# Window-cache copies as 64 quarter parts issued from ScalarE's program, row reads left to GpSimd's queue

## The chip, the cores and the metric

One core of a Trainium2 chip runs the whole kernel. The metric is the device time in microseconds. The kernel has no second core to wait for, so what is read below is one core's engines and its 16 DMA engines.

## What is computed

The reference is one inference step of a decoder layer on 256 prompt tokens and 8 sample tokens (D = 2048), all in float32:

```
q, k, v, u = RMSNorm(x) @ w_in                    # 12 heads x 64, and 1280 pooled channels
attn = merge over 3 dilated windows; for the samples the keys and values are
       rows of cache_win_k / cache_win_v (8 x 2048 x 768 floats each)
x += [attn | pooled u @ pool_w] @ w_out
x += cross-attention(4 heads x 128) over 256 memory tokens (w_ck, w_cv, w_cq, w_co)
x += MoE: top 1 of 4 groups, top 2 of 8 experts, 32 experts with 3 weights of 4 MB each
outputs: y, the new rows, and win_k_sample / win_v_sample =
         the two caches shifted by one row, the new row behind them
```

What matters here is the last line. Rows 1 to 2047 of each sample's cache are copied to rows 0 to 2046 of the output, from device memory to device memory: 2 x 8 copies of 6.29 MB, 100.6 MB in all. No computation reads these outputs, apart from the new last row, which the sample's score reads back.

## The kernel before

It is written by hand, one program per engine, with semaphores. SyncE (SP) issues all the weights into a ring of two 4 MB slots and a third slot: `big(i)` (L403 to L418) waits until piece i-2 has been used by TensorE (`piece_used`) and then loads piece i. The pieces are w_ck, w_cv, seven of w_in, pool_w, four of w_out, w_cq and w_co. A piece of w_in is loaded as rows of 2,048 bytes, w_co and w_e_down as rows of 8,192 bytes, w_e_gate and w_e_up as rows of 16,384 bytes.

The stages of TensorE's program, in order: transposes of the memory tokens and of x; the projection onto w_ck and w_cv (`project`, L668, sample rows L674); five pieces of w_in with `project`; then `channels(j)` (L742) for ten groups of channels, between which the prompt's attention runs pair by pair (scores L771, `turn_probs` L780, values L789); the samples' values (L873) and the pooling map (L863); sixteen output tiles against w_out (L895), each with a transpose of a sample's memory keys (L902); cross-attention (L914 to L980); the projection onto w_co (L1014) with the router; and then 32 experts (`expert(i)`, L1054 to L1138). The experts' weights are used once each. An expert's gate and up weights lie in the two ring slots, and those of the next expert can be loaded into a slot only when TensorE has used it.

GpSimd issues everything else that comes from the caches, in one queue in which transfers start in the order of issue. `window_rows` (L557 to L562) reads the 321 rows of one sample that attention needs, `key_rows(b)` (double buffered) and `value_rows(b)` (three buffers) call it, `memory_rows` (L578) reads 256 rows of a memory cache, and `cache_copy(i)` (L551 to L555) copies one sample's keys or values as 96 rows of 65,504 bytes:

```
src = a[("cache_win_k", "cache_win_v")[kv]][0, b, 1:WB].rearrange("s h e -> (s h e)")
pool.dma_start(dst.rearrange("(p f) -> p f", p=96), src.rearrange("(p f) -> p f", p=96)).then_inc(copied, 16)
```

The order in GpSimd's program is written out by hand: five copies, each when another weight piece has landed (`piece_landed`); then the key rows of samples 0 and 1; and from there on a copy after every second or third batch of rows, again behind a wait for a landed piece. So a batch of rows can stand in the queue behind a copy that was issued just before it. VectorE's `sample_scores(b)` (L1526 to L1530) waits for a batch of key rows; it stands between `enter(p)` and `normalise(p)`, for which TensorE's `turn_probs(p)` waits.

ScalarE issues no DMA. It evacuates banks, squares and takes exponentials; its order against TensorE is set by `A_ORDER`, VectorE's by `V_ORDER` (four banks each).

Of the kernel before, what the change touches and what calls it, by code (L numbers as in the profile page):

```python
# [11 lines left out]
ALU = mybir.AluOpType  # L12
# [120 lines left out]
V_ORDER = (["gains"] + ["mem"] * 8 + ["bias"] * 2 + ["scale"] + ["ck", "cv", "in", "in"] + ["flip"] * 6 + ["in"] * 3  # L133
           + ["score"] * 12 + ["sscore"] * 2 + ["state", "svals"] + ["out"] * KT + ["cq"] * 4 + ["xscore"] * 4
           + ["xsscore", "ssum", "logits", "pos"])
A_ORDER = (["x"] * 16 + ["ck", "cv"] + ["mk"] * 2 + ["in", "sin"] * 5
# [12 lines left out]
def hybrid_decoder_layer(nc, a):  # L149
    with ExitStack() as ctx:  # L150
# [168 lines left out]
        copied = sem("copied")  # L319
# [81 lines left out]
        def _(sp):  # L401
# [29 lines left out]
            for dst, src in ((rb[0:NBUCKET], a["rel_bias"]), (ohp[0:33], cc("ohp", 33)), (ohs[0:33], cc("ohs", 33)),  # L431
                             (tri[:], cc("tri")), (flip, cc("flip")), (moec[:], cc("moe")), (corr[:], cc("corr")),
                             (poolsc[:].rearrange("p g b -> p (g b)"), cc("pools")), (sel[:], cc("sel"))):
                sp.dma_start(dst, src).then_inc(const_landed, 16)  # L434
            sp.wait_ge(zeros_ready, 1)
            for i in range(4):
                sp.dma_start(rbs[0:NBUCKET, i, 0:H], a["rel_bias"]).then_inc(const_landed, 16)
            for i, g in enumerate(("q_norm_g", "k_norm_g")):
                sp.dma_start(gqk[:, i, :], a[g].to_broadcast([P, HD])).then_inc(const_landed, 16)
            sp.dma_start(gck[:, 0, :], a["ck_norm_g"].to_broadcast([P, XD])).then_inc(const_landed, 16)  # L440
            sp.dma_start(b36[:, 0:NG], a["b_rg"].to_broadcast([P, NG])).then_inc(const_landed, 16)
            sp.dma_start(gE[:], a["norm_ffn_g"][0].rearrange("(p k) -> p k", k=KT)).then_inc(const_landed, 16)
# [98 lines left out]
            sp.wait_ge(copied, (2 * NB + 1) * 16)  # L541
# [7 lines left out]
        def _(pool):  # L549

            def cache_copy(i):  # L551
                b, kv = i // 2, i % 2
                src = a[("cache_win_k", "cache_win_v")[kv]][0, b, 1:WB].rearrange("s h e -> (s h e)")
                dst = a[("win_k_sample", "win_v_sample")[kv]][0, b, 0:WB - 1].rearrange("s h e -> (s h e)")
                pool.dma_start(dst.rearrange("(p f) -> p f", p=96), src.rearrange("(p f) -> p f", p=96)).then_inc(copied, 16)  # L555
# [24 lines left out]
            for i in range(5):  # L580
                piece_landed(pool, CV + i)
                cache_copy(i)
# [13 lines left out]
            piece_landed(pool, IN0 + 6)  # L596
            cache_copy(7)
            key_rows(7)
# [6 lines left out]
            piece_landed(pool, POOLW)  # L605
            pool.wait_ge(state_landed, 16)
            cache_copy(8)
            for b in range(3, NB):
                value_rows(b)
            pool.dma_start(a["pool_sample"][0, :, 0:HIST - 1], a["state_pool"][0, :, 1:HIST]).then_inc(copied, 16)  # L610
# [24 lines left out]
            for i in range(14, 16):  # L635
                pool.wait_ge(gu_landed[0], 32)
                cache_copy(i)
# [1316 lines left out]
```

## Time and profile before

| | |
|---|---|
| time, median of 3 runs | 1636.61 us (1635.2 to 1639.62) |
| the profiled execution's own time | 1635.73 us |
| its span, first to last instruction | 1633.9 us |
| busy: TensorE, VectorE, ScalarE, GpSimd | 1262.8, 559.4, 190.1, 58.7 us |
| DMA: bytes, mean rate | 608.79 MB, 373 GB/s |

The span is that of one profiled execution, and the sum of the prediction is made against that execution's time. Busy times overlap each other. In the views below a DMA share is the mean busy share of the 16 DMA engines; it can come out a few per cent above 1, because records that start inside a stretch are counted whole and short ones overlap. The "chain" follows the work that ended last back through what released it, in order of time.

### The profile page before, as it was taken

The page shows a single profiled execution, that of the slowest core. Times are in us where ns is not written, and L with a number is a line of the kernel's source. Part 1 is how long each engine was busy: PE and PEld are TensorE (multiplying, and loading weights), DVE is VectorE, ACT ScalarE, POOL GpSimd, SP SyncE. Part 2 cuts the span into 40 slices and gives each one's busy share as a digit, 9 for nine tenths or more (in the row PEclk, how much of TensorE's full clock was granted, in tenths as well). Part 3 has the DMA queues.
Part 4 walks back from the last instruction along what each step waited for, and adds up shares of the span by engine and source line. Part 5 has one row for each costly group of instructions (what it writes and reads, how often), then busy time and mean ns, then how long its engine had stood idle before and what let it go on. Part 6 is the DMA issues. An engine that isn't in the chain of part 4 may idle for free.

```text
span 1633.9 us, 23554 instructions
## 1 busy us (share of the span) xinstructions
PE 1262.8 (77%) x10061; PEld 654.2 (40%) x10061; DVE 559.4 (34%) x1154; ACT 190.1 (12%) x463; POOL 58.7 (4%) x109
## 2 busy tenths in 40 slices
PE   5999997579998789777777767767767676777676
PEld 3444466465777676432222222222222222222222
DVE  2200153453000142444333433333334343343444
ACT  4000012221110122300000000000000000000000
POOL 0000021112110000000000000000000000000000
PEclk8999998788999899889898998998989899899898
DMA  8999899999889699989999999999999999999995
GB/s 317 308 338 309 309 330 354 313 289 293 286 313 331 228 349 379 356 334 405 428 426 425 428 427 425 426 426 427 428 424 427 426 427 427 424 428 427 425 427 238
DMA packets 85187, 608.79 MB, mean 373 GB/s; under 512 B 10914, under 2 KB 14523, under 8 KB 49529
## 3 DMA queue, kind: packets, MB, share of 16 engines
q1 hardware_dynamic: 76521, 479.68, 72.1%
q0 software_dynamic: 8624, 128.51, 23.4%
q8 instruction: 32, 0.52, 0.1%
q14 instruction: 10, 0.08, 0.0%
HBM read 603.15 MB, written 106.18 MB: 434 GB/s over the span
## 4 chain that ended last, share of the span: by engine, by line
DMA 55%; PE 36%; DVE 4%; SPq 2%; issue 1%; ACT 1%; POOL 0%; DVEq 0%; ACTq 0%
DMA ring<-in_w_e_up_dram 43%; PE pb L1113 11%; PE pb L668 10%; DMA Z<-sample_queries 3%; DMA qkm<-in_cache_mem_k_dram 3%; PE pb L895 3%; DMA ring<-in_w_in_dram 3%; DMA ring<-in_w_out_dram 3%; PE pb L914 2%; PE pb L1014 2%; SPq L434 1%; PE pb L863 1%; PE pb L742 1%; PE pb L674 1%; SPq L494 1%
## 5 line engine op out<-in xcount | busy, mean ns | idle before, releaser
L1113 PE MATMUL pb<-ring,xT 128*32 128x256 f32 x4096 | 312.0, 472 | 196.4 <-DMA ring<-in_w_e_up_dram 195.8
L1884 DVE TENSOR_TENSOR Z<-pb,Z 128x512 f32<-128x512 f32 (+1 forms) x384 | 237.6, 679 | 390.3 <-PE pb L1078 390.3
L1113 PEld LDWEIGHTS pb<-ring,xT 128*32 128x32 f32 x4096 | 154.3, 134 | 377.3 <-DMA ring<-in_w_e_up_dram 246.9
L668 PE MATMUL pb<-ring,hreg 128*128 128x512 f32 (+1 forms) x320 | 125.3, 551 | 0.0
L1138 PE MATMUL pb<-ring,xT 128*32 128x512 f32 x992 | 112.9, 595 | 0.0
L1078 PE MATMUL pb<-xT 32*128 32x512 f32 (+1 forms) x768 | 106.0, 622 | 3.6 <-issue 1.9
L1054 PE MATMUL pb<-Z,xT 128*32 128x512 f32 (+1 forms) x792 | 100.5, 622 | 3.0 <-DVE xT L1863 3.0
L742 PE MATMUL pb<-hreg,ring 128*128 128x264 f32 x320 | 77.2, 402 | 10.9 <-DMA ring<-in_w_in_dram 10.9
L668 PEld LDWEIGHTS pb<-ring,hreg 128*128 128x128 f32 x320 | 60.3, 190 | 61.9 <-issue 60.2
L895 PE MATMUL pb<-hreg,ring 128*128 128x264 f32 x320 | 78.1, 402 | 0.3 <-ACT Z L1307 0.3
L742 PEld LDWEIGHTS pb<-hreg,ring 128*128 128x128 f32 x320 | 62.7, 199 | 24.5 <-DMA ring<-in_w_in_dram 11.3
L1408 ACT ACTIVATE xT<-pb 128x128 f32<-128x128 f32 x32 | 8.9, 278 | 524.9 <-PE pb L1113 524.9
L895 PEld LDWEIGHTS pb<-hreg,ring 128*128 128x128 f32 x320 | 62.6, 200 | 11.1 <-issue 0.4
L1896 DVE TENSOR_SCALAR xT<-xT 128x128 f32<-128x128 f32 x32 | 7.3, 227 | 158.4 <-ACT xT L1408 158.4
L668 PE MATMUL pb<-ring 128*128 128x512 f32 x128 | 57.7, 614 | 0.0
L1657 DVE TENSOR_TENSOR xT<-pb,xT 128x264 f32<-128x264 f32 x16 | 6.9, 433 | 134.9 <-PE pb L895 134.9
L1138 PEld LDWEIGHTS pb<-ring,xT 128*32 128x32 f32 x992 | 29.1, 109 | 56.3 <-issue 55.6
L895 PE MATMUL pb<-Z,ring 128*128 128x264 f32 x192 | 45.3, 386 | 0.0
L1054 PEld LDWEIGHTS pb<-Z,xT 128*32 128x32 f32 (+1 forms) x792 | 19.3, 109 | 57.5 <-issue 53.6
L1119 PE MATMUL pb<-ident,xT 128*128 128x128 f32 x32 | 10.5, 328 | 40.9 <-DVE xT L1902 40.9
L1062 PE MATMUL pb<-ident,xT 128*128 128x128 f32 x132 | 21.2, 284 | 26.1 <-ACT xT L1404 26.1
L895 PEld LDWEIGHTS pb<-Z,ring 128*128 128x128 f32 x192 | 36.5, 190 | 6.2
(302 smaller groups left out, 1059.9 us busy)
## 6 DMA issues: line engine op xcount, KB each, us to landing
ring<-in_w_e_gate_dram SPq DMA_DIRECT2D x64, 2048.0 KB, 19.0
ring<-in_w_e_up_dram SPq DMA_DIRECT2D x64, 2048.0 KB, 23.5
ring<-in_w_e_down_dram SPq DMA_DIRECT2D x31, 4096.0 KB, 22.0
out_win_k_sample_dram<-in_cache_win_k_dram POOLq DMA_DIRECT2D x8, 6141.0 KB, 23.9
out_win_v_sample_dram<-in_cache_win_v_dram POOLq DMA_DIRECT2D x8, 6141.0 KB, 22.2
ring<-in_w_in_dram SPq DMA_DIRECT2D x7, 4096.0 KB, 22.3
ring<-in_w_out_dram SPq DMA_DIRECT2D x4, 4096.0 KB, 22.2
ring<-in_cache_win_k_dram POOLq DMA_DIRECT2D x16, 288.0 KB, 19.1
```

The source lines that it names most:

```text
L434: sp.dma_start(dst, src).then_inc(const_landed, 16)
L668: last = mm(bk[:, 0:n], xt[:, k, tile * P:tile * P + P], w[:, k, 0:n], start=(k == 0), stop=(k == KT - 1))
L742: last = mm(bk[:, 0:TOK], w[:, k, :], hT[:, k, :], start=(k == 0), stop=(k == KT - 1))
L895: last = mm(bk[:, 0:TOK], w[:, k, :], mix(k), start=(i == 0), stop=(i == KT - 1))
L914: last = mm(bk[:, 0:TOK], wk(CQ)[:, k, XD * h:XD * h + XD], hT[:, k, :], start=(k == 0), stop=(k == KT - 1))
L1014: last = mm(pb[o % 4][:, 0:TOK], wo[:, h, P * o:P * o + P], oT[:, h, :], start=(h == 0), stop=(h == XH - 1))
L1054: last = mm(pb[0][32 * c:32 * c + 32, :], pick[0:n, t, :], xn[0:n, t, 512 * c:512 * c + 512], start=(t == 0), stop=(t == 2))
L1062: last = nc.tensor.transpose(pb[0][:, P * j:P * j + P], xe[:, P * j:P * j + P], ident[:])
L1078: last = mm(banks[c][0:n, :], GT[r, P * t:P * t + n], yo[r, :], start=True, stop=True)
L1113: last = mm(pb[1][32 * c:32 * c + 32, 0:256], XT[:, k % 4, 32 * (k // 4):32 * (k // 4) + 32], w[:, :, k8, P * c:P * c + P], start=(k == 0) ...
L1138: last = mm(pb[3][32 * c:32 * c + 32, :], aT[:, 32 * f:32 * f + 32], w[f][:, 512 * c:512 * c + 512], start=(f == 0), stop=(f == 3))
L1884: last = V.tensor_tensor(d, banks[c][0:n, :], d, ALU.add)
```

## The change

All the cache copies leave GpSimd's program. They are cut in quarters: 64 parts, each 32 rows of 49,128 bytes (1.57 MB), contiguous in source and destination, and are issued from ScalarE's program, with no wait of their own, at points that are spread over everything before the experts:

```diff
+            def cache_part(n=1):
+                nonlocal parts
+                for _ in range(n):
+                    b, kv, q = parts // 8, parts // 4 % 2, parts % 4
+                    parts += 1
...
+                    r = slice((WB - 1) * AW // 4 * q, (WB - 1) * AW // 4 * (q + 1))
+                    act.dma_start(dst[r].rearrange("(p f) -> p f", p=32), src[r].rearrange("(p f) -> p f", p=32)).then_inc(copied, 16)
```

The places are: 1 part after the first w_ck tile is evacuated, 2 within the sixteen copies of x, 2 after w_cv's tile, 1 after the memory keys; 4 per w_in piece for n = 0 to 3 (two after `in`, two after `sin`) and 2 for n = 4; 6 in `channels` (j = 1, 2, 3, 5, 7, 9); 2 in the map loop; 13 in the output loop; 9 in cross-attention; 8 in the loop over w_co's tiles, and 2 behind the last `rows_back`.

GpSimd's program keeps its row reads in the same order and with the same waits as before, less the copies and the waits for pieces. At its start it gets the 18 small constant loads that were SyncE's:

```diff
             for t in range(2):
                 sp.dma_start(memr[:, t], a["mem_prompt"][0, P * t:P * t + P]).then_inc(mem_landed[t], 16)
+            big(CK)
             for t in range(2):
                 sp.dma_start(xraw[:, t], a["x_prompt"][0, P * t:P * t + P]).then_inc(x_landed[t], 16)
             sp.dma_start(xraw[0:NB, 2], a["x_sample"][:, 0]).then_inc(x_landed[2], 16)
-            big(CK)
-            for dst, src in ((rb[0:NBUCKET], a["rel_bias"]), (ohp[0:33], cc("ohp", 33)), (ohs[0:33], cc("ohs", 33)),
...
             big(CV)
```
```diff
-            for i in range(5):
-                piece_landed(pool, CV + i)
-                cache_copy(i)
+            for dst, src in ((rb[0:NBUCKET], a["rel_bias"]), (ohp[0:33], cc("ohp", 33)), (ohs[0:33], cc("ohs", 33)),
...
             pool.wait_ge(pads_ready, 1)
             pool.wait_ge(mem_stored, 2 * 16)
             pool.wait_ge(sample_stored, 2 * 16)
             key_rows(0)
             key_rows(1)
-            piece_landed(pool, IN0 + 4)
-            cache_copy(5)
-            key_rows(2)
-            key_rows(3)
-            piece_landed(pool, IN0 + 5)
-            cache_copy(6)
-            for b in range(4, 7):
+            for b in range(2, NB):
                 key_rows(b)
```

The start is put in another order too. w_ck is loaded right behind the memory tokens and before x, w_cv right behind x, and TensorE projects onto w_ck before it transposes x:

```diff
+            pe.wait_ge(v_freed, v_at("mem", 7))
+            memory(CK, "ck")
             for t in range(3):
                 pe.wait_ge(x_landed[t], 16)
             for k in range(KT):
...
-            for i, name in ((CK, "ck"), (CV, "cv")):
...
+            memory(CV, "cv")
```

`V_ORDER` and `A_ORDER` move "ck" ahead of "bias" and of "x", and ScalarE's and VectorE's programs follow: the memory tokens' scale is made before that of x, and the bias and constants come after VectorE's w_ck tile. At the end of its program SyncE waits for 64 parts in `copied` and for the pooling history in a semaphore of its own.

## Rows read from the trace of the kernel before

**Rows 1.** The page: what the DMA engines moved, in 40 slices.

```profile
GB/s 317 308 338 309 309 330 354 313 289 293 286 313 331 228 349 379 356 334 405 428 426 425 428 427 425 426 426 427 428 424 427 426 427 427 424 428 427 425 427 238
```

**Rows 2.** The chain that ended last, among the experts: start, us, what.

```profile
865.21 3.71 PE pb L1113 x64
869.49 25.19 DMA ring<-in_w_e_up_dram
894.72 3.71 PE pb L1113 x64
```

**Rows 3.** Stretches: us, busy of each engine (count), PE clock, DMA share, GB/s.

```profile
0.00:97.81 97.81, 78.06 (x228) 40.11 (x229) 23.09 (x57) 22.06 (x37) 1.36 (x6) 0.91 0.93 315
97.81:228.09 130.28, 130.28 (x781) 64.19 (x781) 26.31 (x29) 12.15 (x28) 7.37 (x14) 1.00 0.91 313
228.09:422.51 194.42, 153.39 (x933) 112.29 (x931) 76.65 (x143) 36.37 (x117) 37.71 (x70) 0.88 0.97 309
422.51:569.83 147.32, 127.85 (x582) 107.51 (x582) 15.48 (x36) 17.03 (x36) 10.71 (x16) 0.94 0.85 298
569.83:701.56 131.73, 113.45 (x702) 77.97 (x706) 51.46 (x157) 35.36 (x86) 1.54 (x3) 0.88 0.91 342
701.56:1608.00 906.44, 646.32 (x6740) 248.39 (x6736) 351.97 (x709) 65.05 (x155) 0.00 (x0) 0.90 1.01 424
```

**Rows 4.** The DMA view of 40 to 103 us, in which two copies run.

```profile
q0 software_dynamic: 208, 12.58, 59.7%
```

**Rows 5.** The DMA view of 278 to 290 us: queue, packets, MB, share.

```profile
q0 software_dynamic: 64, 4.19, 100.0%
q1 hardware_dynamic: 64, 0.13, 3.0%
```

**Rows 6.** A copy among GpSimd's issues: start us, us, instruction, its idle time before.

```profile
272.82 0.53 POOL L555 DMA_DIRECT2D out_win_k_sample_dram<-in_cache_win_k_dram  x1 [30.98 <-DMA ring<-in_w_in_dram]
```

**Rows 7.** The chain that ended last, in the stages before the experts.

```profile
39.30 57.64 PE pb L668 x128
...
228.09 44.44 DMA ring<-in_w_in_dram
...
275.39 27.73 DMA Z<-sample_queries
...
321.64 21.34 DMA Z<-sample_queries
...
439.09 23.70 DMA qkm<-in_cache_mem_k_dram
```

**Rows 8.** What engines waited for, 228 to 423 us: total, times, longest.

```profile
DVE ring L1528 <- DMA Z<-sample_queries: 42.2, 4, 18.6
...
PE pb L780 <- DVEq L1569: 25.9, 2, 17.7
...
PE pb L742 <- DMA ring<-in_w_in_dram: 10.9, 1, 10.9
```

**Rows 9.** The same, 423 to 570 us.

```profile
PE pb L902 <- DMA qkm<-in_cache_mem_k_dram: 14.6, 3, 6.4
```

**Rows 10.** SyncE's issues in order of time: start us, us, instruction.

```profile
6.25 0.39 SPq L418 DMA_DIRECT2D ring<-in_w_ck_dram  x1
6.68 12.29 SPq L434 DMA_DIRECT2D psm<-in_rel_bias_dram  x1
...
244.51 18.66 SPq L474 DMA_DIRECT2D out_win_v_prompt_dram<-Z  x1
```

**Rows 11.** ScalarE in order of time: its sixteen copies of x's transposes.

```profile
18.24 8.21 ACT L1196 COPY xT<-pb 128x264 f32<-128x264 f32 x16 [4.13 <-PE pb L694]
```

**Rows 12.** Short stretches, columns as in rows 3: weights alone, rows with weights, no copy.

```profile
107.00:114.00 7.00, 7.00 (x105) 4.24 (x107) 0.00 (x0) 0.59 (x1) 0.00 (x0) 1.00 1.05 395
...
296.00:308.00 12.00, 0.00 (x0) 0.00 (x0) 4.82 (x2) 0.00 (x0) 0.00 (x0) 0.54 1.03 305
...
553.00:563.00 10.00, 10.00 (x49) 8.55 (x48) 0.77 (x2) 0.90 (x2) 0.00 (x0) 1.00 0.01 2
```

More of the change, by code:

```diff
@@ L625, in _ @@
                     memory_rows(1, b, xv[b], xv_landed)
-                if b in (3, 5):
-                    piece_landed(pool, WOUT + (b + 1) // 2)
-                    cache_copy(9 + (b - 1) // 2)
             pool.wait_ge(v_filled, v_at("out", KT - 1))
             memory_rows(1, 7, xv[7], xv_landed)
-            piece_landed(pool, CQ)
-            cache_copy(12)
-            piece_landed(pool, CO)
-            cache_copy(13)
-            for i in range(14, 16):
-                pool.wait_ge(gu_landed[0], 32)
-                cache_copy(i)
         @block.tensor
@@ L687, in _, with memory @@
                 last.then_inc(v_filled, 1)
+            def memory(i, name):
+                piece_landed(pe, i)
+                project(hmT, wk(i), 0, abank(name), a_filled)
+                project(hmT, wk(i), 1, vbank(name), v_filled)
+            pe.wait_ge(v_freed, v_at("mem", 7))
+            memory(CK, "ck")
             for t in range(3):
@@ L1194, in _ @@
                 square(hreg[:, D * t:D * t + D], memr[:, t], accum_out=st[:, 12 + t:13 + t])
-            for k in range(KT):
-                freed(copy(xT[:, k, :], filled("x")[:, 0:TOK]))
+            roots(st[:, 15:17], st[:, 18:20])
             for t in range(3):
                 n = P if t < 2 else NB
+                act.wait_ge(x_landed[t], 16)
                 act.wait_ge(squared, nsq - 1)
                 square(hreg[0:n, D * (t % 2):D * (t % 2) + D], xraw[0:n, t], accum_out=st[0:n, t:t + 1])
-            roots(st[:, 15:17], st[:, 18:20])
             roots(st[:, 3:6], st[:, 6:9])
@@ L1205, in _ @@
             freed(nc.scalar.mul(mk[:, 0, :], filled("ck")[:, :], st[:, 21:22]))
-            act.wait_ge(a_freed, na)
+            cache_part()
+            for k in range(KT):
+                freed(copy(xT[:, k, :], filled("x")[:, 0:TOK]))
+                if k % 8 == 7:
+                    cache_part()
+            act.wait_ge(a_freed, a_at("ck"))
             act.wait_ge(v_freed, v_at("ck"))
@@ L1225, in _ @@
                 freed(copy(z[:, 0, 512 * n:512 * n + width], filled("in")[:, 0:width]))
+                cache_part(2 if n < 4 else 1)
                 bk, w = filled("sin"), width // 4
@@ L1229, in _ @@
                 freed(last)
+                cache_part(2 if n < 4 else 1)
             def channels(j):
                 freed(copy(uT[:, j, PAD:UW], filled("u")[:, 0:TOK]))
+                if j in (1, 2, 3, 5, 7, 9):
+                    cache_part()
             def channel_rows(first, end):
@@ L1348, in _ @@
             query_square(0)
+            cache_part()
             query_square(1)
+            cache_part()
             query_root(0)
             query_square(2)
+            cache_part()
             query_root(1)
@@ L1355, in _ @@
             query_root(3)
+            cache_part()
             cross_exps(0)
@@ L1395, in _ @@
             rows_back(3)
+            cache_part(2)
+            assert parts == 8 * NB, parts
             act.wait_ge(exp_in, 1)
@@ L1493, in _ @@
                          gT[:, KT + 2 * j:KT + 2 * j + 2].unsqueeze(2).to_broadcast([P, 2, NM]), ALU.mult))
+            dve.wait_ge(squared, 2)
+            mean_root(st[:, 12:14], st[:, 15:17], st[:, 18:20], st[:, 21:23], D)
+            dve.nop().then_inc(scales_ready, 1)
+            nsq = 5
+            dve.wait_ge(squared, nsq)
+            mean_root(st[:, 0:3], st[:, 3:6], st[:, 6:9], st[:, 9:12], D)
+            for t in range(3):
+                last = V.tensor_scalar(dg[:, t, :], ident[:], st[:, 9 + t:10 + t], None, ALU.mult)
+            last.then_inc(diag_ready, 1)
+            freed(V.tensor_scalar(mk[:, 1, :], filled("ck")[:, :], st[:, 22:23], None, ALU.mult))
             dve.wait_ge(const_landed, 16 * N_CONST)
@@ L1497, in _ @@
             V.tensor_scalar(gqk[:, 0, :], gqk[:, 0, :], -HD ** -0.5, None, ALU.mult)
-            nsq = 5
-            dve.wait_ge(squared, nsq)
-            mean_root(st[:, 12:14], st[:, 15:17], st[:, 18:20], st[:, 21:23], D)
-            dve.nop().then_inc(scales_ready, 1)
-            mean_root(st[:, 0:3], st[:, 3:6], st[:, 6:9], st[:, 9:12], D)
-            for t in range(3):
-                last = V.tensor_scalar(dg[:, t, :], ident[:], st[:, 9 + t:10 + t], None, ALU.mult)
-            last.then_inc(diag_ready, 1)
             freed(V.tensor_copy(rbc[:], filled("scale")[:, 0:TOK]))
@@ L1510, in _ @@
             V.memset(uT[:, :, 0:PAD], 0.0)
-            freed(V.tensor_scalar(mk[:, 1, :], filled("ck")[:, :], st[:, 22:23], None, ALU.mult))
-            dve.wait_ge(v_freed, nv)
             for t in range(2):
```

65 lines of the change are left out of this document (33 added, 32 removed).

## The prediction, on record before the changed kernel ran

> **What bounds the kernel now.** I read the page first: the slices of what the DMA engines moved fall into two halves [rows 1], 290 to 380 GB/s before slice 19 and a steady 425 behind it. The chain says what the second half is: an expert every 29.5 us (894.72 - 865.21), of which 25 us is waiting for the next weights [rows 2]. From 701.56 us on the DMA engines are full [rows 3], nothing of the change lies there, and so the end moves by exactly as much as the start of that loop moves. The loop starts when TensorE has used expert 0's first weights, which hangs on TensorE's program, not on a transfer.
>
> So the question is the first 701.56 us. There the stretches by stage [rows 3] show two things side by side. TensorE is busy 78, 130, 153, 128 and 113 us in stages of 98, 130, 194, 147 and 132 us: 41 us idle in stage 3 (channels and attention), 19.5 in stage 4 (w_out), 18 in stage 5 (cross-attention, w_co, routing), none in stage 2. And the DMA engines' work is .93, .91, .97, .85 and .91 of these, 91 + 119 + 189 + 125 + 120 = 643 us (644 unrounded), so they idle about 58 us. Both limits are near, and the gain can't be above about 58 us, since no byte is removed.
>
> Why TensorE idles in stages 3 and 4 is in the chain [rows 7] and GpSimd's issues [rows 6]. At 272.82 GpSimd issues a copy, and the key rows issued behind it in the same queue land 27.7 us after their last issue (275.39); again at 321.64 (21.3 us), and for the memory keys at 439.09 (23.7 us), where the program issues a copy just ahead of them. The copy is why: two of them take .597 of 63 us, 18.8 us each [rows 4]. While one runs all else stands: in 12 us its queue started 64 packets of 65 KB, SyncE's queue 64 of 2 KB [rows 5], one for one.
>
> **The change, part by part.** A copy is 18.8 us of all 16 engines, a part a quarter, 4.7 us, if its bytes cost the same; 64 parts are 301 us, as before. The rate of 49,128-byte rows has no row here. Bounds from below: the weights' 395 GB/s [rows 12], 4.0 us a part, -46 us of transfer in all; from above: the 305 GB/s of small rows mixed with weights, 5.15 us, +30 us. I take 4.7, the nearest in kind.
>
> *Stage 1, start.* w_ck is issued at about 4.7 instead of 6.25 us and has 2 MB (5 us) less ahead of it; before it landed at about 28, now I expect 24. TensorE's 29 us on w_ck (half of 57.64 [rows 7]) then begin at 24 rather than 39, but x's transposes (8.2 us by ScalarE's copies [rows 11]) and the bias (some 3 us), hidden under that load before, stand between w_ck and w_cv. w_cv's end: 24.5 + 29 + 8.5 + 3 + 28 = 93 against 39.3 + 57.6 = 96.9. But the bias rows' store, and behind it hankel and the first w_in piece, are issued after that bias, about where they were (70), and now meet parts: that piece lands at about 95. Net -2 us. SyncE's wait of 12.29 us behind w_ck [rows 10] goes with the moved loads; the 18 loads cost GpSimd 18 x 0.6 = 11 us, while it waited anyway, and are wanted only at 60.
>
> *Stage 2, w_in.* TensorE is full: 31.3 us a piece. A piece's transfer is 4.19 MB at 395, 10.6 us, and its four parts 18.8: 29.4 of 31.3. It fits, until the keys' rows (10 us) and the memory stores come in. In sum the first two stages want 59 + 57 us of other transfers and 22 parts, 103 us, of 226. I charge TensorE +3 us of waiting for pieces, where it had none (between 0 and +8).
>
> *Stage 3.* Before, four copies (75 us) fell in it, now 10 parts (47 us); the other transfers are 189 - 75 = 114. That is 161 us for a stage of 165. Rows no longer queue behind a copy; at worst two or four quarter parts are in flight, 9 to 19 us shared. VectorE's 42.2 us of waiting for rows and TensorE's 25.9 behind it [rows 8] should mostly go, and the 10.9 for the w_in piece halve. What is late next: that piece, and SyncE's queue at one 2 KB row per 49 KB row of a part. Of 41 us idle I leave 14: -27 us (bounds: -10, -35).
>
> *Stage 4.* TensorE's 14.6 us for memory keys [rows 9] shrinks to a few. Transfers: 125 - 56 (three copies) + 61 (13 parts) = 130 us of 135; the 10 us of empty DMA at 553 to 563 [rows 12] get filled. Of 19.5 us I leave 7.5: -12 us (bounds -3, -16).
>
> *Stage 5.* 19 issues on ScalarE at 0.4 us, the price of SyncE's own [rows 10], are 8 us, in a stage in which the work goes from engine to engine; half of them lie in ScalarE's waits: +4 us. The rest of ScalarE's 64 issues (18 us in all) lie in its idle time: it is busy 12 of 130 us in stage 2. Transfers: 120 - 75 + 19 x 4.7 = 134 us of 132, so the last parts run into the first experts: +2 us of arrears, which the full loop can't take back.
>
> Sum: -2 + 3 - 27 - 12 + 4 + 2 = **-32 us**. The profiled execution took 1635.73, so 1603.7; the runs' median stands 0.9 higher, within their spread. I say 1604. Check against the other limit: the loop would start at 670 with 644 us of transfers before it, 26 idle. That is possible, not roomy.
>
> Two rules of the Trainium skill bear on this. In this trace one 2 KB packet of SyncE's goes by per copy row [rows 5]; "DMA: Bandwidth & Descriptors" (Queues, rings and completion order) has an engine change queues only at packet boundaries, a packet of some 9 to 17 descriptors. By that rule weights would get up to 17 rows per copy row, and stage 2's +3 would be 0; the rows show one for one, so I don't count on it.
>
> **The rivals.** *The engines are full anyway* (chance 0.08). The same 644 us of transfers are only put in another order; what TensorE saves on rows it loses on weight pieces, since parts now reach into every piece's time. For it: stages 3 and 4 are planned at 161 of 165 and 130 of 135. Against: the waits of 21 to 28 us have a copy right ahead of them. Then all 32 us are lost again: 1636. This is what the same page of the Trainium skill says (Rules for kernel authors): spreading DMAs over the issuing engines doesn't help bandwidth, it only saves issue time. By it the time stays at 1636.
>
> *ScalarE stands in its issues* (0.12). SyncE's next issue behind a 4 MB piece of 2 KB rows took 12.29 us, and 18.66 us where rows and a copy ran [rows 10]. If ScalarE's issues wait behind SyncE's piece in the same way, the pairs of parts in stages 2 and 3 hold its evacuations 5 to 10 us. It has 100 us spare in stage 2; but in stages 3 and 4 some five pieces at 3 us reach TensorE: +15 us, 1619.
>
> *A part costs more than a quarter* (0.09), the one that ends slower. Each part is 2 rows per engine instead of 6, and if engines stand about 1 us at each part's start or end, 64 us come on top: 644 + 64 + 22 that stay idle = 730 against 701.6, +28 us: 1664. It decides from (701.6 - 22 - 644) / 64 = 0.56 us a part. Against: each engine has other queues to serve meanwhile.
>
> **How the numbers follow.** My forecast has 0.71: 1604. Its own range is 1588 (stages 3 and 4 give all, and 49 KB rows go a little faster) to 1619. To hold 8 in 10 I take in the rival with ScalarE and the upper price of a part: 1587 to 1629. This kernel's measurement tells 0.3%, 5 us, from no change. Faster: 0.71 + 0.12, less a few cases at the edge, 0.82; same 0.08; slower 0.10.
>
> **What would show it.** Right: no idle of VectorE at L1528 above 10 us in all; the loop at 29.5 us an expert as before, starting near 670; stage 3 near 167 us and stage 4 near 135; DMA share in every stage above .95; ScalarE's issues at 0.4 us. Wrong: issues of many us on ScalarE with its bank copies behind them; TensorE waiting at L668, L742 or L895 for the ring; a DMA share near 1 with fewer GB/s than 330 while parts run; or expert 0 waiting for its second half, which then has parts beside it.

## The result, and the profile after

The changed kernel took 1629.45 us (median of 7 runs, 1626.52 to 1634.77) against 1636.98 us for the kernel before (7 runs, 1635.2 to 1644.14): a ratio of 0.9949, 95% interval 0.9925 to 0.9973. It is 8 us faster where 32 were forecast. The profiled execution took 1632.82 us with a span of 1631.0, so it lies in the slower half of its kernel's runs. Its span is 2.9 us below that of before.

The page first: what the DMA engines moved in 40 slices, and the queues (packets, MB, share of 16 engines over the span). q1 is SyncE's, q0 GpSimd's, and q10, ScalarE's, is new.

```profile
GB/s 316 176 343 336 296 321 329 321 246 254 329 341 355 340 309 357 367 387 425 426 428 424 427 428 425 427 425 428 426 425 428 425 426 428 424 427 427 424 428 257
q1 hardware_dynamic: 74609, 479.21, 72.2%
q10 hardware_dynamic: 3072, 100.62, 16.6%
q0 software_dynamic: 7408, 28.37, 5.7%
```

The change does what it says: the 100.62 MB of copies are in q10. A part took 0.166 x 1631 / 64 = 4.2 us of all engines, against the 4.7 taken. But beside [rows 1] the second slice (41 to 82 us) has fallen from 308 to 176 GB/s, and new dips of 246 and 254 stand in the ninth and tenth (326 to 408 us). The copies left the places where they stood in the way, and in three places too little came in for them.

The stretches by stage of after, cut at the same landmarks of TensorE's program as [rows 3] (stretch, its length, busy us of TensorE, its weight loads, VectorE, ScalarE, GpSimd with counts, clock, DMA share, GB/s). The first ends within TensorE's wait for the first w_in piece, which begins at 95.88 us, the last but one is TensorE's wait for expert 0's second half and its work on it, the last is the loop.

```profile
0.00:96.90 96.90, 75.40 (x227) 38.58 (x227) 23.54 (x58) 22.96 (x38) 9.83 (x22) 0.95 0.80 266
96.90:237.90 141.00, 132.23 (x780) 65.06 (x781) 25.72 (x29) 11.58 (x26) 5.27 (x10) 0.96 0.92 318
237.90:425.58 187.68, 152.13 (x934) 110.84 (x932) 76.64 (x143) 36.18 (x117) 36.03 (x67) 0.88 0.85 283
425.58:555.54 129.96, 122.49 (x582) 104.14 (x582) 15.48 (x36) 18.14 (x36) 8.67 (x12) 0.99 0.93 353
555.54:688.50 132.96, 112.64 (x694) 77.48 (x694) 51.28 (x157) 35.83 (x86) 0.00 (x0) 0.89 0.93 345
688.50:704.76 16.26, 6.01 (x64) 2.72 (x64) 0.81 (x4) 0.00 (x0) 0.00 (x0) 0.69 1.01 428
704.76:1605.00 900.24, 642.64 (x6676) 245.75 (x6680) 351.31 (x705) 65.05 (x155) 0.00 (x0) 0.90 1.00 424
```

What TensorE waited for before the loop (engine, line, releaser: total us, times, longest), and VectorE's waits for rows (L1540 is L1528 of before):

```profile
PE pb L714 <- DMA ring<-in_w_in_dram: 26.2, 1, 26.2
PE pb L1085 <- DMA ring<-in_w_e_up_dram: 10.2, 1, 10.2
PE pb L636 <- issue: 9.8, 1, 9.8
```
```profile
DVE ring L1540 <- DMA Z<-sample_queries: 25.9, 3, 17.2
```

The waits that the change was to remove have shrunk or gone: VectorE's 42.2 us for rows [rows 8] are 25.9, TensorE's 25.9 us behind it are not in the list any more, nor are the 14.6 us for memory keys [rows 9]. In their place stand three waits of TensorE for weights: 9.8 us for the first w_in piece (the list names no releaser for it), 26.2 us for a later one (10.9 before [rows 8]), and 10.2 us for the second half of expert 0, which there was not. At 688.50 us TensorE has used expert 0's first half, 13.1 us earlier than before (701.56); when it has used the second half, at 704.76, it is level with before (705.01). Both times are read from SyncE's issues of expert 1's halves, which wait for just that. A fourth wait, 8.4 us for w_ck, comes with the new start and was in the forecast.

### The profile page after: what moved, and what is told of

It is laid out like the page before. It is cut to its first block, busy times and chain, and to the rows that moved or that the text cites. A ratio compares the mean times of both kernels' runs of the same rounds, so it can differ in the third digit from the quotient of the medians.

```text
span 1631.0 us, 23603 instructions
## 1 busy us (share of the span) xinstructions
PE 1257.0 (77%) x10061; PEld 648.3 (40%) x10061; DVE 559.3 (34%) x1154; ACT 191.8 (12%) x463; POOL 59.8 (4%) x111
## 3 DMA queue, kind: packets, MB, share of 16 engines
q10 hardware_dynamic: 3072, 100.62, 16.6%
## 4 chain that ended last, share of the span: by engine, by line
DMA 51%; PE 42%; another core or an unknown queue 2%; DVE 2%; issue 2%; SPq 1%; ACT 1%; POOL 0%; DVEq 0%; ACTq 0%
DMA ring<-in_w_e_up_dram 46%; PE pb L636 11%; PE pb L1085 10%; PE pb L867 5%; PE pb L714 4%; DMA ring<-in_w_out_dram 2%; PE pb L886 2%; PE pb L986 2%; DMA ring<-Z 2%; DMA ring<-in_w_ck_dram 1%; PE pb L642 1%; SPq L482 1%; PE pb L845 1%; PE pb L835 1%
## 5 line engine op out<-in xcount | busy, mean ns | idle before, releaser
L714 PE MATMUL pb<-hreg,ring 128*128 128x264 f32 x320 | 76.5, 399 | 26.2 <-DMA ring<-in_w_in_dram 26.2
L714 PEld LDWEIGHTS pb<-hreg,ring 128*128 128x128 f32 x320 | 62.2, 197 | 39.0 <-DMA ring<-in_w_in_dram 26.6
L867 PE MATMUL pb<-hreg,ring 128*128 128x264 f32 x320 | 74.0, 387 | 2.7 <-DMA ring<-in_w_out_dram 2.4
L867 PEld LDWEIGHTS pb<-hreg,ring 128*128 128x128 f32 x320 | 59.5, 190 | 12.3 <-DMA ring<-in_w_out_dram 2.6
L636 PEld LDWEIGHTS pb<-ring 128*128 128x128 f32 x128 | 24.9, 196 | 39.5 <-issue 39.5
```

The source lines that it names most:

```text
L636: last = mm(bk[:, 0:n], xt[:, k, tile * P:tile * P + P], w[:, k, 0:n], start=(k == 0), stop=(k == KT - 1))
L714: last = mm(bk[:, 0:TOK], w[:, k, :], hT[:, k, :], start=(k == 0), stop=(k == KT - 1))
L867: last = mm(bk[:, 0:TOK], w[:, k, :], mix(k), start=(i == 0), stop=(i == KT - 1))
```

## The experiments

Two theories went in. **A, placement**: bytes and prices are about right, but the parts are issued in bunches and in wrong places, so that they take the engines from a weight piece which TensorE needs, while elsewhere the engines stand empty. **B, the engines are full anyway**: whatever order is chosen, the time stays. Beside them: the start's new order costs or gives something by itself; long rows are to blame; and the part's lower price is from its size or from its queue. Ratios are against the kernel before on the same chip; the kernel before took 1634.72 to 1639.71 us on the chips used, so kernels are compared by ratios where a few us matter. In the recorded expectations theory C is this document's B, and "theory B" of the first two is the one on the start's new order.

### The copies left out, in either kernel

`e1_after_no_copies` is after without its 64 parts, `e2_before_no_copies` is before without its 16 copies:

```diff
-                    act.dma_start(dst[r].rearrange("(p f) -> p f", p=32), ...).then_inc(copied, 16)
```
```diff
-                pool.dma_start(dst.rearrange("(p f) -> p f", p=96), ...).then_inc(copied, 16)
+                pass
```

> The changed kernel without its 64 parts: the window caches' shifted copies are left out, all else as it is. Theory A (what is lost of the forecast is lost to parts that stand in the way of weight pieces): without them TensorE's stages run at their own speed, stage 3 near 165 us and the wait of 26 us for the w_in piece goes, the first w_in piece is there in time; about 1570 to 1580 us. Theory B (the new start order and the moved constants cost by themselves): the 8 us that the first stage grew by stay, TensorE still waits near 10 us before the first w_in piece, and this kernel is slower than the old one without copies.

> The old kernel without its 16 copies (left out; the pooling history is still copied). It gives the price of the copies in the old order, 1637 less this. Theory A: 1575 to 1585 us, at least 3 us above the changed kernel without parts, whose start order is shorter by that. Theory B: equal to it or below it.

Measured: 1574.36 us, ratio 0.9606 [0.9582, 0.9629], and 1571.22 us, 0.9594 [0.9572, 0.9615]. So the copies cost 1636.98 - 1571.22 = 66 us in the old order and 1629.45 - 1574.36 = 55 us in the new one. There is much to gain, and the new order takes a sixth of it. And the other half of the change, the new start, gives nothing by itself: without any copies the two kernels can't be told apart, where at least 3 us for the new start were expected. TensorE begins on w_ck at 27.05 us instead of 39.29, but x's transposes then stand between w_ck and w_cv, and it begins on the first w_in piece at 95.92 us against 97.22. That is the order of events which the prediction's first step had.

### Row length

`e3_after_rows_16k` and `e4_after_rows_8k` cut a part into 96 and 192 rows in place of 32:

```diff
-... dst[r].rearrange("(p f) -> p f", p=32), src[r].rearrange("(p f) -> p f", p=32) ...
+... dst[r].rearrange("(p f) -> p f", p=96), src[r].rearrange("(p f) -> p f", p=96) ...
```

> The changed kernel, each part as 96 rows of 16,376 bytes instead of 32 of 49,128; same bytes, same places. Theory A, with queues served one packet each in turn: while parts run a 2 KB row of a weight piece goes by every 0.7 us instead of every 2.1 per engine, so the w_in piece that landed 60 us after its issue lands in under 45, and expert 0's second half in under 30 instead of 37: 5 to 15 us off, 1614 to 1624. Theory C (the engines are simply full, order does not matter): no change within 3 us, 1629, or slower by the shorter rows' price, some us.

> As before with 192 rows of 8,188 bytes a part. Theory A: weights' share grows again, the key rows' too, 1610 to 1622, unless the shorter rows cost more time of the engines (8 KB weight rows ran at 25.7 bytes a ns and engine against 26.6 for 16 KB). Theory C: 1629 or slower.

Measured: 1626.58 us (12 runs), 0.994 [0.9917, 0.9963], and 1626.55 us, 0.9937 [0.9913, 0.9961]. Neither tests what it was made for: both have the 3,072 packets of after in ScalarE's queue, for 192 rows

```profile
q10 hardware_dynamic: 3072, 100.62, 16.6%
```

which is 2,048 packets of 49,128 bytes and 1,024 small ones. So contiguous rows were put together again before they moved. They are repeats of after, and as such of use: three measurements of the same transfers give 0.9949, 0.994 and 0.9937. `e5_short_rows` keeps rows of 8,188 bytes apart by handing them out in another order:

```diff
+... src[r].rearrange("(a b f) -> b a f", b=16, f=2047) ...
```

> The changed kernel with each part's access turned so that its rows can't be joined again: 16 x 12 rows of 8,188 bytes, 96 KB apart within an engine's share no more than before (in e3 and e4 the trace showed 2,048 packets of 49,128 bytes as in the changed kernel: the same transfers). Theory A (long rows starve the other queues, one packet each in turn): the w_in piece issued at 238 us lands in under 45 us instead of 60 and TensorE's wait of 26 us for it shrinks to under 15; expert 0's second half lands in under 28 us instead of 37; time 1612 to 1622. Theory C (engines full, only the sum of bytes counts): within 3 us of 1627.

Measured: 1646.15 us, 1.0035 [1.0014, 1.0057]. The queue and two waits of this run:

```profile
q10 hardware_dynamic: 13312, 100.62, 18.6%
```
```profile
PE pb L714 <- DMA ring<-in_w_in_dram: 30.4, 1, 30.4
PE pb L867 <- DMA ring<-in_w_out_dram: 11.7, 2, 8.9
```

Short rows cost a part 0.186 x 1647.9 / 64 = 4.8 us instead of 4.2, and the wait for the w_in piece has not gone; it is longer. Row length decides the shares while parts run, but shorter rows don't bring that piece earlier. Here are the queues of the same stretch, 240 to 262 us, in after and in this run:

```profile
q10 hardware_dynamic: 190, 6.24, 81.8%
q0 software_dynamic: 187, 0.75, 13.8%
q1 hardware_dynamic: 190, 0.58, 6.6%
```
```profile
q10 hardware_dynamic: 541, 4.04, 51.1%
q0 software_dynamic: 543, 2.44, 33.2%
q1 hardware_dynamic: 539, 1.19, 16.9%
```

190, 187 and 190 packets in one, 541, 543 and 539 in the other. The three counts rise and fall together in short stretches too (12, 15 and 14 in 250 to 252 us of after, 22, 20 and 21 in 252 to 254), so each queue sends one packet in turn, and its share of bytes goes by its row size. With rows of 8 KB SyncE's queue moves twice as much in this stretch (1.19 against 0.58 MB), but GpSimd's rows three times, and the parts run longer. What SyncE's queue moves is not yet the w_in piece alone: 0.58 MB in 190 packets are rows of 3,072 bytes, and the piece has rows of 2,048.

### Where the 26 us come from

ScalarE in order of time around the w_in piece (start us, us, instruction, idle time before it):

```profile
215.43 1.48 ACT L1164 ACTIVATE qkm<-Z 128x1536 f32<-128x1536 f32 x1 [3.98 <-DVE Z L1483]
...
226.72 0.52 ACTq L1159 DMA_DIRECT2D out_win_k_sample_dram<-in_cache_win_k_dram  x1
226.96 0.59 ACT L1216 COPY Z<-pb 128x512 f32<-128x512 f32 x1
227.27 0.61 ACTq L1159 DMA_DIRECT2D out_win_k_sample_dram<-in_cache_win_k_dram  x1
...
228.00 0.52 ACTq L1159 DMA_DIRECT2D out_win_v_sample_dram<-in_cache_win_v_dram  x1
...
228.55 0.71 ACTq L1159 DMA_DIRECT2D out_win_v_sample_dram<-in_cache_win_v_dram  x1
...
245.04 0.52 ACTq L1159 DMA_DIRECT2D out_win_v_sample_dram<-in_cache_win_v_dram  x1
...
246.98 0.52 ACTq L1159 DMA_DIRECT2D out_win_v_sample_dram<-in_cache_win_v_dram  x1
```

and SyncE's issues:

```profile
230.95 0.40 SPq L455 DMA_DIRECT2D out_win_k_prompt_dram<-Z  x1
238.12 0.40 SPq L418 DMA_DIRECT2D ring<-in_w_in_dram  x1
266.63 18.01 SPq L462 DMA_DIRECT2D out_win_v_prompt_dram<-Z  x1
```

The program has four parts spread over the fourth w_in piece (n = 3). But in time ScalarE stands in the heads' norms until 226.7 us, evacuates the piece's banks only then, and issues all four within 2 us, then the two of n = 4: six parts in 20 us. They are 25 us of all engines, with GpSimd's key rows beside them.

What they hold up first is not the piece but what stands ahead of it in SyncE's queue: the store of the prompt's keys, issued at 230.95, 256 rows of 3,072 bytes. It gets one row in per 49 KB row of a part and takes 36.2 us from issue to landing. The piece is issued at 238.12, moves its first rows at 262 to 264 us, when the parts are through, and lands at 298 beside GpSimd's rows. Over the runs the wait follows that store:

| kernel | the store of the prompt's keys took | TensorE waited for the piece |
|---|---|---|
| `after` | 36.2 us | 26.2 us |
| `e7_forward` | 35.4 us | 21.8 us |
| `e5_short_rows` | 18.6 us | 30.4 us |
| `e6_unbunched` | 9.5 us | 1.1 us |
| `e1_after_no_copies` | 5.3 us | not in the list |

`e5_short_rows` is the exception: its store is through sooner, but its parts run on beside the piece until 284 us. Whether the piece would be in time with the store issued behind it, and the parts left where they are, was not tried.

The chain that ended last names no releaser for the wait, but TensorE's list above does:

```profile
270.87 0.85 PE pb L743 x8
271.72 26.19 another core or an unknown queue
297.95 10.42 PE pb L714 x32
```

And behind it the engines have little to do: 307 to 338 us and 365 to 377 us of after, columns as in the stretches.

```profile
307.00:338.00 31.00, 31.00 (x174) 24.33 (x172) 22.22 (x45) 11.31 (x41) 5.93 (x12) 1.00 0.59 203
365.00:377.00 12.00, 11.27 (x66) 9.03 (x65) 7.43 (x11) 2.80 (x14) 0.00 (x0) 1.00 0.03 3
```

### One wait at a time

Four kernels each go at one place. `e6_unbunched` gives n = 3 no parts and spreads its four over n = 0 to 2; `e7_forward` moves the eight parts of w_co's loop, which run while expert 0 loads, to channels, the map and the output loop; `e8_start` takes the parts out of x's copies and from behind w_cv; `e9_half_first` lets SyncE issue expert 0's second half ahead of the first half of expert 1's down weights.

```diff
-                cache_part(2 if n < 4 else 1)
+                cache_part((2, 3, 2, 0, 1)[n])
...
-                cache_part(2 if n < 4 else 1)
+                cache_part((3, 3, 3, 0, 1)[n])
```
```diff
-                if j in (1, 2, 3, 5, 7, 9):
+                if j >= 1:
...
-                if j in (3, 7):
+                if j % 2:
...
-                if o % 4 < 3 or o == KT - 1:
+                if o % 4 < 3 or o in (3, 11, KT - 1):
...
-                if o % 2 == 0:
-                    cache_part()
```
```diff
-            cache_part()
+            cache_part(3)
...
-                if k % 8 == 7:
-                    cache_part()
...
-            cache_part(2)
...
-            cache_part()
+            cache_part(3)
```
```diff
-            sp.wait_ge(a_filled, a_at("xval", 3))
-            sp.dma_start(down1[0], w1[:, 0:2]).then_inc(dn1_landed, 16)
             piece_used(sp, CO)
             gate_up(0, 0, 1)
+            sp.wait_ge(a_filled, a_at("xval", 3))
+            sp.dma_start(down1[0], w1[:, 0:2]).then_inc(dn1_landed, 16)
```

> The changed kernel with the four parts of w_in piece 3 issued with pieces 0 to 2 (5, 6, 5, 0, 2 parts instead of 4, 4, 4, 4, 2). Theory A: the 26 us wait for the w_in piece came from six parts issued within 20 us (226 to 247), because ScalarE's program stands in the heads' norms before piece 3; with two left there the wait falls under 12 us and the time by 10 to 15 us, to 1612 to 1618. Rival D (that piece would be late anyway, its SyncE issue waits for the heads' stores and it shares with the key rows): wait above 18 us, time 1622 or more.

> The changed kernel with the 8 parts of the w_co loop issued earlier: 3 more in channels (j = 4, 6, 8), 3 more in the map loop, 2 more in the output loop. Theory A: the parts hold back SyncE's queue from 600 to 684 us, so that expert 0's second half comes 15 us late; now it is there within 20 us of its issue, the expert loop starts 8 to 14 us earlier, and the earlier stages, whose DMA engines idled 30 us, lose under 4: 1616 to 1622. Theory C: the loss moves to the earlier stages whole, 1625 to 1630.

> The changed kernel with the six parts of the start placed so that the bias store and the first w_in piece meet none: 3 behind the first w_ck tile, none within x's copies or behind w_cv's tile, 3 behind the memory keys. Theory A: TensorE's 10 us before the first w_in piece shrink to under 3 and with them the whole by 6 to 9 us, to 1618 to 1622. Rival: the piece is late because its issue stands behind the bias store, which TensorE's new order puts at 66 us; then 5 us or more of the wait stay.

> The changed kernel with one edit in SyncE's program: the first half of expert 1's down weights (2 MB, wanted only after 715 us) is issued behind expert 0's second gate/up half instead of ahead of it. Theory A (SyncE's queue is first in, first out and gets one packet per packet of a part, so what stands ahead of the half costs it far more than its bytes): the half lands in under 28 us instead of 37 and the 10 to 15 us wait falls under 5, but the parts and bytes are the same, so the DMA-full expert loop gives part of it back: 3 to 8 us off, 1620 to 1625. Theory C (only the sum of bytes before the loop counts): the wait goes, and the loop's first weights are as much later, time within 2 us of 1628.

| kernel | us | ratio | wait it aimed at | what came for it |
|---|---|---|---|---|
| `e6_unbunched` | 1629.32 | 0.9939 [0.9913, 0.9965] | w_in, 26.2 to 1.1 us | 16.2 us for an earlier w_in piece |
| `e7_forward` | 1630.98 | 0.9955 [0.9933, 0.9977] | expert 0, 10.2 to 4.4 us | 15.3 us for w_out |
| `e8_start` | 1636.80 | 0.9993 [0.9964, 1.0022] | first piece, 9.8 us to none | 14.8 us for the next w_in piece |
| `e9_half_first` | 1631.95 | 0.9946 [0.9921, 0.997] | expert 0, 10.2 to 8.4 us | nothing new; 25.6 us for w_in stay |

The lines of e6, e7 and e8 for it, from the same list of waits:

```profile
PE pb L636 <- DMA ring<-in_w_in_dram: 16.2, 1, 16.2
```
```profile
PE pb L867 <- DMA ring<-in_w_out_dram: 15.3, 1, 15.3
```
```profile
PE pb L636 <- DMA ring<-in_w_in_dram: 14.8, 1, 14.8
```

None beats after, and none reached the time that theory A had expected of it. In the first three the wait aimed at shrank by the expected edit, and another came where the parts went. In `e9_half_first`, where no part moves, the wait hardly shrank (8.4 us, where under 5 were expected). On these four alone theory B would look shown.

### The old order with quarters

`e12_old_order_quarters` is before with each copy as four parts in a row, still in GpSimd's queue:

```diff
+                for q in range(4):
+                    r = slice((WB - 1) * AW // 4 * q, (WB - 1) * AW // 4 * (q + 1))
+                    pool.dma_start(dst[r].rearrange("(p f) -> p f", p=32), ...).then_inc(copied, 16)
```

> The old kernel with each copy cut in four DMAs of 32 rows of 49,128 bytes, in the same place of GpSimd's queue. It prices the parts by themselves: in the changed kernel the parts took 16.6% of 16 engines' span, 271 us, where the copies took about 300. Theory E (the shorter rows move faster by themselves): the copies' share falls by 2 points, the windows with a copy shorten, and the time falls by 5 to 10 us with no change of order at all, to 1627 to 1632. Rival F (it is the queue, hardware-made descriptors instead of GpSimd's): the share stays and so does 1637.

Measured: 1646.88 us, 1.0049 [1.0024, 1.0075]. The queue, and TensorE's and VectorE's waits:

```profile
q0 software_dynamic: 9904, 128.51, 23.4%
```
```profile
PE pb L904 <- DMA qkm<-in_cache_mem_k_dram: 16.4, 3, 6.9
```
```profile
DVE ring L1530 <- DMA Z<-sample_queries: 60.9, 6, 21.8
```

The queue's share is that of before to the digit, so the part's lower price in after does not come from its size. In GpSimd's queue quarters are worth nothing; rows still stand behind four of them, and wait 60.9 us instead of 42.2 [rows 8]. So what after gained does not come from the cut. It comes from the queue of their own and the new places together; no run has the one without the other.

### Parts where the engines are idle

The idle stretches of after are a table of free places. `e10_parts_in_gaps` moves the four parts of n = 3 there: two to channels (j = 4, 6), two to the map.

```diff
-                cache_part(2 if n < 4 else 1)
+                cache_part((2, 2, 2, 0, 1)[n])
...
-                if j in (1, 2, 3, 5, 7, 9):
+                if j in (1, 2, 3, 4, 5, 6, 7, 9):
...
-                if j in (3, 7):
+                if j in (1, 3, 5, 7):
```

`e13_gaps_start` adds to it a start with parts right behind w_ck and none where the first w_in piece loads, `e14_gaps_half` adds e9's swap, `e11_gaps_start_half` has both:

```diff
-            cache_part()
+            cache_part(3)
...
-                if k % 8 == 7:
-                    cache_part()
...
-            cache_part(2)
...
-                cache_part((2, 2, 2, 0, 1)[n])
+                cache_part((2, 3, 2, 0, 1)[n])
...
-                if j in (1, 2, 3, 4, 5, 6, 7, 9):
+                if j in (1, 2, 3, 4, 5, 6, 7, 8, 9):
```

`e15_start_gap_filled` is e11 with five parts behind w_ck, one behind w_cv and three fewer in w_co's loop:

```diff
-            cache_part(3)
+            cache_part(5)
...
+            cache_part()
...
-                if o % 2 == 0:
+                if o in (0, 3, 6, 9, 12):
```

> The changed kernel with the four parts of w_in piece 3 put where its DMA engines stood idle (channels j = 4 and 6, map j = 1 and 5), pieces 0 to 2 keeping their four each. Theory A: neither the 26 us wait of the channels nor the 16 us wait at w_in piece 2 that e6 put in its place; total idle of the DMA engines before the experts falls by 10 us and the time with it: 1614 to 1620. Theory C: a new wait of the same size turns up at w_out, 1626 or more.

> e10 and e9 together, and a start in which the bias store and first w_in piece meet no part (3 parts behind the first w_ck tile, none in x's copies or behind w_cv's tile, 1 behind the memory keys, one more each at w_in piece 1 and channel 8). Theory A: the gains add, since each takes away idle time of the DMA engines: 1606 to 1614. Theory C: 1624 or more.

> e11 without the changed order of the two SyncE issues: e10 and the start alone. Theory A (each idle stretch of the DMA engines that is filled ahead of the experts pays): the first w_in piece is in time and with it 5 to 8 us against e10, 1612 to 1616; e14 then pays the rest. Theory G (only the order in SyncE's queue pays): within 2 us of e10, 1620.

> e10 with expert 0's second half issued ahead of expert 1's down weights, start as in the changed kernel. Theory A: the half lands 10 us earlier, but the bytes between it and the full loop are the same, so 0 to 4 us against e10, 1616 to 1620. Theory G: all of e11's gain, 1608 to 1612.

> e11 with 3 parts of the w_co loop moved to the start (5 instead of 3 behind the first w_ck tile, 1 behind w_cv's), where the DMA engines idle 30 us of the first 100. Theory A: 3 parts are 12.7 us of engine time; idle before the experts falls by 9 to 12 us, expert 0's weights wait less and the time falls 5 to 10 us below e11, 1600 to 1605. Theory C (what is gained there is lost to the first w_in piece): 1608 or more.

| kernel | us | ratio to before |
|---|---|---|
| `e10_parts_in_gaps` | 1620.15 (1614.48 to 1626.97) | 0.9886 [0.9846, 0.9926] |
| `e13_gaps_start` | 1612.81 (1598.6 to 1618.14) | 0.9851 [0.9814, 0.9887] |
| `e14_gaps_half` | 1610.56 (1602.47 to 1618.75) | 0.9844 [0.9816, 0.9872] |
| `e11_gaps_start_half` | 1609.97 (1605.88 to 1612.79) | 0.9816 [0.9782, 0.985] |
| `e15_start_gap_filled` | 1599.88 (1595.34 to 1604.36) | 0.9798 [0.9774, 0.9821] |

All five are faster than before and have a lower median than after, with the parts, their size and their queue unchanged. The interval of `e10_parts_in_gaps` just touches that of after (0.9925 to 0.9973); the others lie clear of it. `e10_parts_in_gaps` and `e13_gaps_start` move parts alone, the other three also have e9's swap in SyncE's queue. `e15_start_gap_filled` is 2.0% faster than before, four times what the change gave. What it filled: first the stretch up to the loop for before, then the same for after with its hole at 50 to 62 us, then for this kernel, with the two holes of after as it has them.

```profile
0.00:705.01 705.01, 606.42 (x3277) 403.72 (x3277) 193.62 (x424) 122.96 (x303) 58.70 (x109) 0.92 0.92 314
```
```profile
0.00:704.76 704.76, 600.91 (x3277) 398.82 (x3277) 193.48 (x424) 124.69 (x303) 59.80 (x111) 0.92 0.89 316
50.00:62.00 12.00, 12.00 (x48) 6.28 (x46) 0.75 (x1) 3.60 (x10) 0.00 (x0) 1.00 0.00 1
```
```profile
0.00:665.00 665.00, 595.91 (x3277) 396.18 (x3277) 194.39 (x426) 124.56 (x304) 59.59 (x111) 0.95 0.92 333
50.00:62.00 12.00, 12.00 (x51) 6.35 (x49) 0.75 (x1) 4.06 (x11) 0.00 (x0) 1.00 0.99 325
307.00:338.00 31.00, 31.00 (x175) 24.86 (x174) 20.27 (x51) 10.66 (x36) 4.16 (x8) 1.00 1.01 340
```

Before moved 314 GB/s on the way to the loop, after 316, this one 333. The DMA share of after is lower than that of before, .89 against .92: the change made the engines idle more, about 78 us against 56. Its parts took less time (4.2 us instead of the 4.7), and what that freed went into idle time instead of an earlier loop. In `e15_start_gap_filled` they idle 0.08 x 665 = 53 us: of the 40 us by which its loop starts earlier than in after, some 25 are less idle time and the rest less work, since a part took 0.164 x 1593.4 / 64 = 4.1 us.

What stays open here: e11 against e13 and e14 is within the intervals, so whether start and swap add up can't be told. `e13_gaps_start` came where theory A had it (1612 to 1616), but `e14_gaps_half` came where the rival had it, that the order in SyncE's queue gives it all (1608 to 1612), so the swap may be worth more beside filled gaps than alone. Between e11 and e15 three things moved at once (five parts instead of three behind w_ck, one behind w_cv, three fewer in w_co's loop), and which of them pays was not tried.

## Why the prediction was wrong

Stage by stage, with the lengths of [rows 3] and of the stretches after:

| step | forecast | measured |
|---|---|---|
| stage 1, start | -2 | +8 (97.81 to 105.67: 96.90 and 8.8 of waiting) |
| stage 2, w_in | +3 | +2 (130.28 to 132.2, from 105.67 to 237.90) |
| stage 3 | -27 | -7 (194.42 to 187.68) |
| stage 4 | -12 | -17 (147.32 to 129.96) |
| stage 5 | +4 | +1 (131.73 to 132.96) |
| arrears | +2 | +13 at expert 0 (3.45 to 16.26), -3 in the loop |
| sum | -32 | -3 in the spans, -8 in the medians |

**Right.** The diagnosis: rows waited because a copy stood ahead of them in their queue, and once the copies had left it they waited less; e12 shows that this is not the cut. But the waits did not "mostly go": VectorE's are 25.9 us, where the prediction's own sign of being right was 10 at most. Stage 4's idle time of TensorE came out as forecast, 19.5 us before and 7.5 after. That the stage gave 17 and not 12 is luck: 5 us are shorter busy time (127.85 to 122.49 for the same 582 matmuls) at a granted clock of 0.99 instead of 0.94, which the sum didn't have. The end moves with the start of the loop. One row per row between queues held at 49 KB and at 8 KB. That w_ck first is worth next to nothing in itself (e1 against e2). And the rival that ScalarE stands in its issues is refuted: they took 0.5 to 0.7 us each, somewhat over the 0.4 taken, none was blocked, and stage 5 lost 1 us rather than 4. So is the rival that a part costs more than a quarter: it costs less, 4.2 us where the sum took 4.7.

**The step that failed is stage 3's**: "10 parts (47 us); the other transfers are 189 - 75 = 114. That is 161 us for a stage of 165." The sum came out, .85 x 187.68 = 160 us of transfers, though partly by luck: a part was cheaper than taken, and parts issued before the stage ran on into it (17.88 MB of copies moved in it, 11.4 parts and not 10). What it doesn't say is when. I set the bytes of a stage against its length and took parts that are spread over the program as spread over time. Six of them came in 20 us, because ScalarE's program runs in steps of its own, and they held up SyncE's queue with the one piece that TensorE needed next; then came 31 us at a share of .59 and 12 at .03. I had named "that piece, and SyncE's queue at one 2 KB row per 49 KB row of a part" as what would be late next, and left 14 us of TensorE's idle time for all; it was 35.6 (187.68 - 152.13), of which that piece is 26.2. Nor did the sum have what stood ahead of the piece in its queue, the store that took 36.2 us. ScalarE's order in time was in the trace of before, and I didn't lay the diff's places on it.

**The second is stage 1**: the piece was expected at about 95 and TensorE could start on it at 105.67 only. Of the parts in x's copies (issued at 60.78 and 64.95 us) the second still ran when the bias rows were stored at 66.34, which were read back at 74.36 and had the piece issued behind them at 74.78, those behind w_cv (81.31 and 81.87) ran beside the piece, and from 50 to 62 us the engines had nothing. e8 removes the wait, and pays for it at the next piece.

**The third is the arrears**: +2 taken, 13 lost at expert 0. SyncE issued the second half at 661.61 us and it was there 37 us later, behind down weights in its own queue (issued at 603.48 and 618.28) which themselves had parts beside them at one row each:

```profile
661.61 37.03 DMA ring<-in_w_e_up_dram
```

I had written that it would show the forecast wrong if expert 0 waited "for its second half, which then has parts beside it", and had only the +2 us of arrears for it in the sum.

**The rival "the engines are full anyway"** came near in time (1636) and is wrong as a cause: the engines were not full, they idled more than before, and with the same bytes in the same queues, and no change but in the places of parts, e13 took 1612.81 (0.9851), and e15, with the swap in SyncE's queue, 1599.88. The Trainium skill says that spreading DMAs over the issuing engines doesn't help bandwidth ("DMA: Bandwidth & Descriptors", Rules for kernel authors). Here the share of time for the same 129 MB went from 23.4% to 16.6 + 5.7, a little better; but that says nothing of waiting: short rows no longer stand behind long copies (VectorE's wait fell from 42.2 to 25.9 us), and copies can be placed by need. The rule of the same page (Queues, rings and completion order) that an engine drains some 9 to 17 descriptors of one queue before it switches isn't borne out, if a packet of the profile is a descriptor: 190, 187 and 190 packets, which rise and fall together within 2 us. The prediction took from that rule that weights would get up to 17 rows per copy row. That follows only if a copy row is a packet by itself, since the rule as stated holds for the copy's rows as well; the chances didn't rest on it.

**The size forecast was right for the mechanism, not for this placement.** -32 us was called possible since 26 us of idle time would be left. With better places and e9's swap TensorE had used expert 0's first half at 660.21 us and the second at 663.66 (e15), where the prediction had the loop start at 670; after had it at 688.50 and 704.76. Part of that is luck with a size: the sum counted 4.7 us a part, and at e15's 4.1 the 64 parts are some 38 us less work.

## What to carry to other kernels

A transfer that nobody waits for is free only while the DMA engines are idle, so its place is not evenly over the program but the idle stretches of the trace: list the stretches with a low DMA share, see which instruction of the issuing engine runs just before each, and put it there, not where a weight piece, or what stands ahead of it in its queue, is under way and wanted next. Bytes per stage against the stage's length is only a first bound; lay each issue on the issuing engine's own timeline, since an engine that catches up issues everything at once. And when closing one wait at a time gains nothing, look at whether the idle time of the shared resource fell: e6 to e9 gained nothing one by one, and a move into idle time took the ratio from 0.9949 to 0.9886, and further ones with the swap to 0.9798.

## What the runs showed of the hardware that I had not expected

- A DMA from memory to memory whose rows are contiguous is cut anew: 32, 96 and 192 rows gave the same 2,048 packets of 49,128 bytes. Only rows out of order stayed short.
- Three queues at once take turns packet by packet (190, 187, 190; and 541, 543, 539 in 22 us), a software queue among them, with rows of 3 KB beside rows of 49 KB. So a short store can stand long: 0.79 MB took 36.2 us beside six parts and 5.3 us with no copies, and the w_in piece behind it in the queue stood with it.
- The same bytes took less time in after than in e12, with packets of the same size: 16.6 + 5.7 = 22.3% of the span against 23.4%. That the queue is the cause is not shown: within ScalarE's queue the places of the parts alone take the share from 16.6% (after) to 16.1% (e7).
- Issues on ScalarE are not held up by SyncE's queue: 0.5 to 0.7 us beside a SyncE issue that stood for 18.01 us.
- Shorter rows within the parts made the kernel about 1% slower than its repeats (ratios 1.0035 against 0.994 and 0.9937): 4.8 against 4.2 us a part.
